# The order of VectorE's work at a layer boundary and the place of a wait for a spill, in an fp32-split GEMM trunk

## The reference

```python
for l in range(DEPTH):
    hn = rms_norm(x, p['norm_mix_pre'][l])
    mix, ... = even_mixer(hn, ...) if l % 2 == 0 else odd_mixer(hn, ...)
    x = x + rms_norm(mix, p['norm_mix_post'][l])
    hn = rms_norm(x, p['norm_ffn_pre'][l])
    x = x + rms_norm(swiglu(hn, p['w_ffn_in'][l], p['w_ffn_out'][l]), p['norm_ffn_post'][l])
```

## Time and profile before

| | |
|---|---|
| median of 3 runs (lowest, highest) | 3627.06 us (3624.95, 3628.56) |
| the profiled execution | 3623.46 us |
| its span, first to last instruction | 3621.5 us |
| mean granted TensorE clock | 0.948 |
| PE busy | 3384.6 us, 93% |
| VectorE busy | 1915.4 us, 53% |
| ACT busy | 1253.8 us, 35% |
| GpSimd busy | 457.1 us, 13% |
| chain that ended last, by engine | PE 86%, DVE 8%, ACT 3%, issue 2% |
| HBM traffic over the span | 131 GB/s |

### The profile page before, as it was taken

One profiled execution on the slowest core, in us unless ns is written; L12 is line 12 of the kernel. 1 busy time (PEld: TensorE's weight loads), 2 busy tenths in 40 slices (PEclk: granted clock), 3 DMA queues, 4 the chain that ended last, 5 costly groups with the idle time before them and its releaser, 6 DMA issues.

```text
span 3621.5 us, 61189 instructions
## 1 busy us (share of the span) xinstructions
PE 3384.6 (93%) x24672; PEld 3260.6 (90%) x24672; DVE 1915.4 (53%) x2317; ACT 1253.8 (35%) x1582; POOL 457.1 (13%) x400
## 2 busy tenths in 40 slices
PE   8999996858989999999999799998989999999997
PEld 8998885846989999999999799985989999999997
DVE  5446667485555553355544566914465543455544
ACT  5344443131443332233333435321443332233332
POOL 0027773000000000000000035920000000000000
PEclk9999996979999999999999899976999999999999
DMA  6543331000534454445444544532535444454543
GB/s 202 150 140 109 120 108 44 4 24 16 163 111 151 145 158 150 133 151 151 148 156 137 169 146 122 171 134 116 157 106 155 147 153 151 137 151 145 158 151 109
DMA packets 118661, 474.88 MB, mean 131 GB/s; under 512 B 13424, under 2 KB 15088, under 8 KB 115568
## 3 DMA queue, kind: packets, MB, share of 16 engines
q1 hardware_dynamic: 108864, 421.58, 37.7%
q10 hardware_dynamic: 9648, 51.17, 3.7%
HBM read 450.66 MB, written 22.03 MB: 131 GB/s over the span
## 4 chain that ended last, share of the span: by engine, by line
PE 86%; DVE 8%; ACT 3%; issue 2%; POOL 1%; DMA 1%; ACTq 0%; DVEq 0%; POOLq 0%
PE ps L348 49%; PE ps L352 24%; PE ps L1839 1%; PE ps L1859 1%; ACT w_hi L288 1%; DVE w_lo L296 1%; DVE X L520 1%; PE ps L1413 1%; PE ps L954 1%; DVE M L517 1%; ACT M L501 1%; PE ps L317 1%; PE ps L1362 1%; PE ps L932 1%; PE ps L312 0%
## 5 line engine op out<-in xcount | busy, mean ns | idle before, releaser
L348 PE MATMUL ps<-x_hi,w_hi 128*128 128x320 f32 x4768 | 1428.8, 313 | 44.7 <-DVE x_lo L545 28.7
L288 ACT ACTIVATE w_hi<-raw 128x1024 fp32r<-128x1024 f32 (+1 forms) x756 | 841.6, 1114 | 1746.5 <-PE ps L352 1694.1
L348 PE MATMUL ps<-x_lo,w_hi 128*128 128x320 f32 x4768 | 1419.9, 311 | 0.0
L296 DVE TENSOR_TENSOR w_lo<-raw,w_hi 128x1024 fp32r<-128x1024 f32 (+1 forms) x640 | 834.4, 1306 | 837.2 <-ACT w_hi L288 824.7
L348 PEld LDWEIGHTS ps<-x_hi,w_hi 128*128 128x128 f32 x4768 | 905.7, 190 | 53.4 <-issue 30.7
L348 PEld LDWEIGHTS ps<-x_lo,w_hi 128*128 128x128 f32 x4768 | 905.8, 190 | 0.9
L352 PE MATMUL ps<-x_hi,w_lo 128*128 128x320 f32 x4768 | 800.6, 310 | 10.0 <-POOL w_lo L296 9.8
L352 PEld LDWEIGHTS ps<-x_hi,w_lo 128*128 128x128 f32 x4768 | 726.6, 189 | 13.3 <-POOL w_lo L296 12.7
L296 POOL TENSOR_TENSOR w_lo<-raw,w_hi 128x1024 fp32r<-128x1024 f32 x116 | 301.9, 2609 | 1715.8 <-ACT w_hi L288 1713.9
L348 PE MATMUL ps<-u_hi,w_hi 128*128 128x320 f32 x1408 | 417.7, 311 | 8.3 <-DVE u_lo L607 8.3
L348 PE MATMUL ps<-u_lo,w_hi 128*128 128x320 f32 x1408 | 417.1, 310 | 0.0
(11 more groups left out here) (374 smaller groups left out, 2874.8 us busy)
## 6 DMA issues: line engine op xcount, KB each, us to landing
raw<-in_w_ffn_in SPq DMA_DIRECT2D x352, 512.0 KB, 3.6
raw<-in_w_ffn_out SPq DMA_DIRECT2D x128, 704.0 KB, 4.1
raw<-in_w_in_even SPq DMA_DIRECT2D x116, 512.0 KB, 3.6
raw<-in_w_in_odd SPq DMA_DIRECT2D x96, 512.0 KB, 3.6
raw<-in_w_out_even SPq DMA_DIRECT2D x32, 512.0 KB, 3.6
raw<-in_w_out_odd SPq DMA_DIRECT2D x32, 512.0 KB, 3.6
hS<-in_state_hgrn ACTq DMA_DIRECT2D x4, 1024.0 KB, 5.1
out_hgrn_s<-hS ACTq DMA_DIRECT2D x4, 1024.0 KB, 5.1
```

The lines of the kernel that those rows point to most:

```text
L288: nc.scalar.activation(w_hi[s % 2][:, 0:g.kt, :], raw[s % 4][:, 0:g.kt, :], ACT.Copy)\
L296: eng.tensor_tensor(w_lo[s % 2][:, 0:g.kt, :], raw[s % 4][:, 0:g.kt, :], w_hi[s % 2][:, 0:g.kt, :].bitcast(f32), sub).then_inc(sem(f"split ...
L348: nc.tensor.matmul(out, w_hi[s % 2][:, k, :], x[:, kk, :], start=half == 0 and k == 0 and x is xh, stop=False)
```

## The change

In `boundary_dve` the `split_lo` of unit c moves one step later, behind the residual of c+1 and the `x_lo` of c: six splits, of units 2 to 7, now at c = 3 to 8. The order on VectorE was residual c, x_lo c-1, split c; it becomes residual c, x_lo c-1, split c-1. This holds at all four boundaries with a product behind them. In the block of ACT the wait for the spill, the two waits beside it and the five loads of constants move from the place ahead of `act_lead` into it, behind the `split_hi` of the 15th unit of in_c (unit 14, counted from 0).

```diff
-        def act_lead(act, g, n):
+        def act_lead(act, g, n, late=None):
 
             def body(i, s):
                 split_hi(act, i, s)
                 if s - g.unit0 == 12:
                     root_act(act, n)
+                if s - g.unit0 == 14 and late:
+                    late()
             steps(act, g, body, skip=8)
@@ boundary_dve
-                if HEAD <= c < 8 and g is not None:
-                    split_lo(dve, "dve", 0, g.unit0 + c)
+                if HEAD < c and g is not None:
+                    split_lo(dve, "dve", 0, g.unit0 + c - 1)
@@ block.scalar
             act.dma_start(x_spill, X[:, :, :]).then_inc(sem("spilled"), 16)
-            act.wait_ge(sem("spilled"), 16)
-            act.wait_ge(sem("x_lo"), 24)
-            act.wait_ge(sem("norm_sq"), 24)
-            for dst, src in ((odc[:, :], "odc"), (cv_in[:, :, :, :], "conv_in"), (h_in[:, :, :], "h_in"),
-                             (w_a[:, :, :, :], "w_a"), (w_x[:, :, :, :], "w_x")):
-                act.dma_start(dst, d[src]).then_inc(sem("odd_consts"), 16)
-            act_lead(act, plan["in_c"], 4)
+
+            def odd_constants():
+                act.wait_ge(sem("spilled"), 16)
+                act.wait_ge(sem("x_lo"), 24)
+                act.wait_ge(sem("norm_sq"), 24)
+                for dst, src in ((odc[:, :], "odc"), (cv_in[:, :, :, :], "conv_in"), (h_in[:, :, :], "h_in"),
+                                 (w_a[:, :, :, :], "w_a"), (w_x[:, :, :, :], "w_x")):
+                    act.dma_start(dst, d[src]).then_inc(sem("odd_consts"), 16)
+            act_lead(act, plan["in_c"], 4, odd_constants)
```

## The result

The changed kernel takes 3571.33 us in the median of 4 runs (3568.65 to 3573.96), the kernel before, run beside it, 3626.26 us (4 runs); the ratio is 0.9848, 95% interval 0.9836 to 0.9860. That is 54.9 us less, where 38.5 were forecast, and the median lies 12 us under 3583, the low end of the range. The profiled execution took 3568.65 us against 3623.46, 54.8 us less; its span is 3566.6 us, the mean granted clock 0.957 (0.948 before).

The account below looks back on a forecast made before the run. The prediction took PE as the bound, at 3.52 us a lead unit once boundary waits go. 10.05 + 9.70 + 9.70 + 9.22 - 0.19 = 38.48 us less takes the median from 3627.06 to 3588.6 us, range 3583 to 3600.

Parts of the forecast that it names:

- The first edit: New VectorE order at boundaries: seven units take 24.64 us, saving 10.05 at up00, 9.70 at in_c and at up10.
- VectorE's series of 3.47: VectorE's instructions of one boundary step in series, 3.47 us, just under PE's 3.52 us a unit.
- the ring over two steps: ACT and VectorE waiting for each other at boundaries: the same 5.68 us now over two steps, 2.84 us a step.
- the 1.1 us worked out for the residual: Spare time at boundaries: residual c+2 ends about 4.0 us after the reference moment, ACT wants it at 5.1 us.
- The second edit: Spill wait moved behind in_c's boundary: ninth unit 3.52 us in place of 12.74, saving 9.22; eleventh unit loses 0.19.
- the paragraph on DMA: Store and constant loads under running matmuls in in_c: weight loads have 11.7 us, even 7.1 fits; cost 0.
- The sum: Whole kernel: four local terms total 38.48 us, taking the median from 3627.06 to 3588.6.
- (b): Rival: 1.2 GHz stretches at the boundaries stay though idle goes, 6.3 us less gain, 3594.9; chance 0.06.
- (a): Rival: VectorE or ACT sets the boundary step, 3.97 us with 0.25 us hand-overs; 8.1 us less gain, 3596.7; chance 0.09.
- (c): Rival: store and constants starve the weight loads behind in_c's boundary, PE stalls; 7.5 us less gain, 3596.1; chance 0.07.
- (d): Rival: a wait keeps boundary steps at 5.7 us; only 9.0 us gained, 3618.0; chance 0.02.
- (e): Rival: PE stays at 1.2 GHz through the lead units, 6.38 us each; 21.6 us slower, 3648.7; chance 0.02.

Follow-up runs that it names:

- dve_extra: Changed kernel with one more 640-column subtraction per step on VectorE, ahead of x_lo, at the three boundaries with a residual; 3594.93 us.
- repeat_after: The changed kernel run again, with nothing altered; 3574.20 us in 4 runs, ratio 0.9856 to the kernel before.
- repeat_before: The kernel before the change run again, with nothing altered; 3627.85 us in 10 runs.
- spill_only: The kernel before with only the spill wait and constant loads moved, old VectorE order kept; median 3600.81 us in 6 runs, ratio 0.9930.
- pad12_again: Second run of the changed kernel with 12 extra matmuls ahead of the retention stage; 3565.37 us, ratio 0.9846 to the kernel before.
- pad_after_6: Changed kernel with 6 extra matmuls, about 0.88 us, ahead of the retention stage; 3583.93 us.

## Why the prediction was wrong

**The first edit: right in each figure.** 10.05, 9.70 and 9.70 us at the three boundaries, nothing at in_a, nothing at the last. PE's 3.52 us sets the step, VectorE's series of 3.47 fits under it, and the ring over two steps never shows. The fine point was too careful: the spare time behind VectorE is larger than the 1.1 us worked out for the residual, as `dve_extra` shows.

**The second edit: right.** 9.22 us for the ninth unit, and 0.20 for the eleventh where 0.19 stood. The constants were free at their new place. The prediction counted with a ring load of 7.1 us; beside the constants they took 8.7 in the median and 9.3 at the most, and stayed within the 11.7 us. Two times in the paragraph on DMA are off by its own terms: with 28.8 us gone ahead of it, the first reader at 2132.51 moves to about 2104, not 2113 (measured 2098.59, the even mixer's 5 us among the difference), and the last constant landed at 2048.9, not 2059. Neither enters the sum.

**The sum: here it failed.** It took everything outside the boundaries as fixed: "the median goes from 3627.06 to 3588.6" adds four local terms to the time of the whole. The runs showed that the odd mixer, the same instructions in the same order, takes 378.7, 385.5, 396.5, 402.2 or 410.8 us (the extra matmuls taken as they are), by where it begins against the grant's changes. The change moved it from the 396 to 402 of the kernel before to 385.5. The term that was left out is 11.05 us of odd mixer in the two profiles (16.4 us with all that lies outside the costed stretches) and about 15 in the medians: 53.6 us between the medians of the rounds with `repeat_after` (3627.84 in 15 runs of before, 3574.20), less 38.5. Rival (b) had the clock in it, but only at the boundaries, and as a loss. The figures to bound the missing term stood in the trace of before: the chain's 16.7 us for a state update at 1.2 GHz beside the 9.25 us (4.17 + 1.27 + 3.81, the first with a part at the lower clock) of the next head; the stage has four heads.

**What was chance.** The 5.23 us of the even mixer and the +1.11 at the start were chance. The even mixer took between 667.4 and 675.6 us over the profiles, with no relation to the kernel, and 667.4, 673.9 and 672.9 in three executions of the changed one. The 1.49 us ahead of down00 are another matter of place and not of luck. PE begins down00's first unit after a pause of 2.07 us, at 1.2 GHz in the first profile of before and at 2.4 GHz in `repeat_before`. The shorter time came in all 13 profiles with the new order, and in one of the four with the old. That the forecast missed by 16.4 us and not by more was luck as well: over the variants the odd mixer spans 34 us.

**The rivals.** (a), (c), (d) and (e) did not occur. (b) did not either: the dips went with the waits, clock 1.00. The 0.25 us for a hand-over in (a) stands in no row; from the end of `split_hi` to the start of `split_lo` it is 0.10 us (14.38 + 1.04 to 15.52 in the earlier trace rows), and 0.10 after the change (1039.88 + 1.06 to 1041.04).

**What stays open.** It is not shown why most executions of one kernel meet the grant's changes in the same way. Not all do: the kernel before took two courses in two profiles, one run in six went a dear way in `spill_only` and in `pad12_again`, and one in four of `pad_after_6` a cheap way. What the traces show is where the place is set. In the ten profiles with both edits and an unchanged boundary, the third split of in_d comes 115.08 to 115.12 us after the grant's last rise, which falls in in_c's first unit, though the even mixer ahead of it took anything from 667.4 to 674.0 us. Where the pause behind in_c is left in, the last rise falls in the ninth unit instead, and the distance is 86.7 to 88.2 us; in `spill_only` it is 98.2, in `dve_extra` 115.35, and two extra matmuls ahead of the stage add 0.29 us behind it. So each edit, and even a quarter of a microsecond at a boundary, gives the stage another place. Why PE's start in in_c's first unit comes so nearly at the same distance ahead of the rise each time is open.

## What to carry to other kernels

Sum local terms for the edited places, and then ask which other stages run partly at the lower TensorE clock: their time can move by tens of us with the moment at which they begin (here by up to 34). A change of 1.5% that touches nothing there owed near a third of its size to such terms, and one of a few us could owe them its sign. To tell the two apart, cut both profiles at the same instructions and compare stretch by stretch, or run the kernel with a fraction of a microsecond of useless work ahead of such a stage; a total alone would have credited 15 us to five useless matmuls or charged 20 us to VectorE. In a ring of two engines, letting one run a step ahead costs no instruction; here it took the step from 5.68 us to PE's own 3.52 (the 2.84 us worked out for the ring itself stayed hidden under PE).

## What was not expected of the hardware

Dense work does not by itself raise the clock. In the kernel before PE is busy without a gap through 16.7 us of state update and stays at 0.50 (the window has two entries of its neighbours):

```profile
2409.58:2426.26 16.68, 16.68 (x22) 0.50 0.00 0
```

Against that, the lead units are at 1.00 from their second unit on. The Trainium skill (TensorE: Matmul & The Clock Gate, What's actually happening) says that activity releases the throttle; here time counted as busy was not enough.

The Trainium skill (TensorE: Matmul & The Clock Gate, What's actually happening) also calls the number of cold matmuls variable from run to run of the same kernel. The even mixer agrees (667.4, 673.9 and 672.9 us in three executions of the changed kernel), and so does the odd mixer of the kernel before (396.54 and 402.17). The odd mixer of the changed kernel does not: the same three executions have it at 385.49, 385.49 and 385.41 us, with the first fall of the clock in the retention stage in the same microsecond of the stage. The windows of 1 us around it, in the first profile:

```profile
2358.00:2359.00 1.00, 1.00 (x11) 0.97 0.43 147
2359.00:2360.00 1.00, 1.00 (x6) 0.50 0.99 410
```

and in `repeat_after`, where the whole is 6.31 us later:

```profile
2364.31:2365.31 1.00, 1.00 (x10) 0.98 0.52 180
2365.31:2366.31 1.00, 1.00 (x7) 0.50 0.94 393
```
